# Neighbourhood attention of the last block: projection, head norm and attention woven together by pairs of heads

## The chip, the core and the metric

The kernel runs on one core of a Trainium2 chip. The metric is the device time of one launch in microseconds (us). The core has a matrix engine (TensorE, "PE" in the profile; "PEld" is its loading of stationary operands), a vector engine (DVE), an activation engine (ACT), a general engine (POOL) and a queue that issues transfers (SP). Each engine runs its own instructions in the order in which they were written; between engines only semaphores keep order. An instruction that waits on a semaphore holds up everything behind it on its engine. TensorE runs at one of two granted clocks, 2.4 or 1.2 GHz; the profile shows them as 1.00 and 0.50.

## What is computed

Two blocks of two layers each, on 512 tokens of 1024 features. The change lies in the last of the four layers: a neighbourhood attention of 16 heads with 64 features, on a grid of 64 columns by 8 rows. Each query sees a window of 16 grid columns and 256 context tokens. Cut to what matters:

```
q = rms(heads(hx @ w[:, :hd]), g_q);   k = rms(heads(hx @ w[:, hd:2*hd]), g_k);   v = heads(hx @ w[:, 2*hd:])
k_c = rms(heads(hc @ w[:, hd:2*hd]), g_k);   v_c = heads(hc @ w[:, 2*hd:])
s = [q . k_window * d**-0.5 + bias,  q . k_c * d**-0.5]        # softmax over both parts together
x = x + gx1 * (softmax(s) @ [v_window, v_c]) @ w_out
```

`rms` divides each head by the root of its mean square plus 1e-6 and multiplies by a gain.

## The kernel before

**Jobs.** Activations stand transposed, features on the 128 partitions, tokens along the row. A job is one output tile of 128 features: eight tiles k of the 1024 input features, and for each k three matmuls (high by high, high by low, low by high part, since every fp32 number is split in two fp32r halves) of 512 columns. Key and value jobs have three more of 256 columns for the context tokens. The weights of a job arrive by one transfer (`RAW`, two buffers), ACT rounds them to the high half (`round_hi`, buffer `WH`, four slots), POOL subtracts to the low half (`lo`, `WL`), PE waits for `lo_done`.

**Order of the last layer's attention.** `plan()` gives three phases of eight jobs, `na_q`, `na_k`, `na_v`, all streamed by `stream` (L1293 the 512 columns, L1295 the 256). The head norm of a finished tile is woven into later jobs: ACT squares it (L604), PE sums squares over a head with a matmul by `HALF` (`head_norm_pe`, L1273, L1276), ACT takes the root (L607, L609), DVE inverts and scales (L1587, L1589). PE turns each value tile by nine transposes (`v_turn`, L1264). Only then `neighbourhood_pe` runs the attention: 64 steps, a step being one head and 128 queries. A step has scores (L1200: three matmuls of 256 columns against local keys and three against context keys), four transposes of the numerators (`turn`, L1208) and the product with the values (`av`, L1221: four tiles, 128 columns each although a head has 64). Between them DVE adds the bias (L1804), takes the maximum (L1808), the reciprocal (L1813) and scales the result (`store`, L1818); ACT copies the context scores (L635), takes the exponential (L641) and evicts the turned numerators (L662) to `PTN`, of which there are two buffers, as there are two PSUM banks for scores, for turning and for results.

**After it.** `turn_out` turns all eight output tiles (L1008), ACT and DVE split them in halves (L667, L1834), and phase `res2` of eight jobs forms the product with `w_out`. Its first matmuls can begin at once, since the weights of its first four jobs are there.

## Time and profile before

| | us |
|---|---|
| median of 3 runs (3108.92 to 3121.93) | 3110.72 |
| profiled execution, as timed | 3116.66 |
| its span, first to last instruction | 3114.9 |
| PE busy in the span | 2893.2 (93%) |
| DVE, ACT, POOL busy | 1642.5, 1134.9, 1096.9 |

Busy means that an instruction was executing. Matmuls overlap, and their ends are modelled, so the cost of a matmul in a dense row is the distance between two starts, not its duration. The granted clock was 0.969 on average. The part that the change touches runs from the first matmul on the layer's normed input to the last of the product with `w_out`.

### The profile page before, as it was taken

The page shows a single profiled execution, that of the slowest core. Times are in us where ns is not written, and L with a number is a line of the kernel's source. Part 1 is how long each engine was busy: PE and PEld are TensorE (multiplying, and loading weights), DVE is VectorE, ACT ScalarE, POOL GpSimd, SP SyncE. Part 2 cuts the span into 40 slices and gives each one's busy share as a digit, 9 for nine tenths or more (in the row PEclk, how much of TensorE's full clock was granted, in tenths as well). Part 3 has the DMA queues.
Part 4 walks back from the last instruction along what each step waited for, and adds up shares of the span by engine and source line. Part 5 has one row for each costly group of instructions (what it writes and reads, how often), then busy time and mean ns, then how long its engine had stood idle before and what let it go on. Part 6 is the DMA issues. An engine that isn't in the chain of part 4 may idle for free.

```text
span 3114.9 us, 39241 instructions
## 1 busy us (share of the span) xinstructions
PE 2893.2 (93%) x14018; PEld 2351.2 (75%) x14018; DVE 1642.5 (53%) x2339; ACT 1134.9 (36%) x1857; POOL 1096.9 (35%) x501
## 2 busy tenths in 40 slices
PE   4998899998998899997999799999979989989998
PEld 3886588886766678874878688888858878868887
DVE  6537696755576788855212416644542565431111
ACT  3333443334464533235212423121243357542222
POOL 2441444445322444452212123233323233234443
PEclk9999899999999899998999899999979989999999
DMA  5350355523421355531111123333312110123222
GB/s 212 122 183 35 121 191 198 192 101 103 136 68 60 112 185 194 172 115 36 61 68 54 41 75 122 122 131 113 134 55 68 55 41 22 33 75 100 95 96 87
DMA packets 90419, 325.47 MB, mean 104 GB/s; under 512 B 10036, under 2 KB 12852, under 8 KB 89784
## 3 DMA queue, kind: packets, MB, share of 16 engines
q1 hardware_dynamic: 85392, 312.21, 29.3%
q10 hardware_dynamic: 4904, 11.68, 1.2%
q8 instruction: 70, 1.15, 0.2%
q14 instruction: 53, 0.43, 0.0%
HBM read 321.75 MB, written 2.10 MB: 104 GB/s over the span
## 4 chain that ended last, share of the span: by engine, by line
PE 83%; DVE 8%; ACT 4%; issue 2%; DMA 1%; POOL 1%; DVEq 0%; ACTq 0%; SPq 0%; POOLq 0%
PE bank L1293 57%; PE junk L1295 9%; PE bank L1076 2%; PE bank L1221 2%; PE bank L1061 1%; PE bank L1208 1%; PE bank L1200 1%; PE bank L1310 1%; PE bank L1180 1%; PE junk L1200 1%; ACT UF L816 1%; ACT Uh L816 1%; DVE ADA L1383 1%; PE bank L1102 1%; DMA ADA<-in_ast 1%
## 5 line engine op out<-in xcount | busy, mean ns | idle before, releaser
L466 POOL TENSOR_TENSOR WL<-RAW,WH 128x1024 fp32r<-128x1024 f32 x392 | 985.9, 2516 | 1793.0 <-ACT WH L760 1280.4
L760 ACT ACTIVATE WH<-RAW 128x1024 fp32r<-128x1024 f32 x292 | 307.3, 1053 | 384.3 <-PE junk L1295 192.0
L1293 PE MATMUL bank<-U1h,WH 128*128 128x512 f32 x960 | 378.0, 394 | 18.3 <-DVE U1l L1631 18.3
L1293 PE MATMUL bank<-Uh,WH 128*128 128x512 f32 x832 | 341.5, 410 | 56.5 <-DVE Ul L1633 56.1
L1293 PE MATMUL bank<-U1l,WH 128*128 128x512 f32 x960 | 375.4, 391 | 0.0
L1293 PE MATMUL bank<-U1h,WL 128*128 128x512 f32 x960 | 375.1, 391 | 0.0
L1293 PE MATMUL bank<-Hh,WH 128*128 128x512 f32 x864 | 340.1, 394 | 11.5 <-DVE Hl L548 11.5
L1293 PE MATMUL bank<-Hl,WH 128*128 128x512 f32 x864 | 340.7, 394 | 0.0
L1293 PE MATMUL bank<-Hh,WL 128*128 128x512 f32 x864 | 339.4, 393 | 0.0
L1293 PE MATMUL bank<-Ul,WH 128*128 128x512 f32 x832 | 333.9, 401 | 0.0
L1293 PE MATMUL bank<-Uh,WL 128*128 128x512 f32 x832 | 332.4, 400 | 0.0
L1483 DVE SCALAR_TENSOR_TENSOR XT<-bank,GATE,XT 128x512 f32 x112 | 84.0, 750 | 369.6 <-PE bank L1293 203.3
L1383 DVE CUSTOM_DVE_ANT_0 ADA<-ADA,CB 128x1024 f32<-128x1024 f32 x128 | 215.1, 1686 | 109.8 <-DMA ADA<-in_ast 98.1
L1293 PEld LDWEIGHTS bank<-Uh,WH 128*128 128x128 f32 x832 | 158.9, 191 | 108.9 <-issue 45.5
L1293 PEld LDWEIGHTS bank<-U1h,WH 128*128 128x128 f32 x960 | 181.0, 189 | 63.3 <-issue 16.1
L1293 PEld LDWEIGHTS bank<-U1h,WL 128*128 128x128 f32 x960 | 181.3, 189 | 38.3
L1293 PEld LDWEIGHTS bank<-U1l,WH 128*128 128x128 f32 x960 | 181.4, 189 | 36.5
L1293 PEld LDWEIGHTS bank<-Hh,WH 128*128 128x128 f32 x864 | 162.8, 188 | 51.4 <-DVE Hl L548 16.0
L1293 PEld LDWEIGHTS bank<-Hh,WL 128*128 128x128 f32 x864 | 162.8, 188 | 37.5
L1293 PEld LDWEIGHTS bank<-Hl,WH 128*128 128x128 f32 x864 | 163.0, 189 | 34.5
L1293 PEld LDWEIGHTS bank<-Uh,WL 128*128 128x128 f32 x832 | 159.6, 192 | 38.0
L1293 PEld LDWEIGHTS bank<-Ul,WH 128*128 128x128 f32 x832 | 159.6, 192 | 34.7
(334 smaller groups left out, 5277.4 us busy)
## 6 DMA issues: line engine op xcount, KB each, us to landing
RAW<-in_wst SPq DMA_DIRECT2D x392, 512.0 KB, 3.4
ADA<-in_ast SPq DMA_DIRECT2D x192, 512.0 KB, 4.5
NST<-in_nstrip ACTq DMA_DIRECT2D x16, 192.0 KB, 2.3
XT<-in_xt SPq DMA_DIRECT2D x1, 2048.0 KB, 15.4
STRIP<-in_strip ACTq DMA_DIRECT2D x8, 256.0 KB, 2.7
CB<-in_cb ACTq DMA_DIRECT2D x4, 512.0 KB, 4.3
DX<-in_dx ACTq DMA_DIRECT2D x1, 2048.0 KB, 8.1
out_xt<-XT SPq DMA_DIRECT2D x1, 2048.0 KB, 7.2
```

The lines of the kernel that those rows point to most:

```text
L466: pool.tensor_tensor(WL[:, s4], RAW[:, s2], WH[:, s4].bitcast(F32), ALU.subtract)\
L760: act.activation(WH[:, c % 4], RAW[:, c % 2], ACT.Copy).then_inc(S("hi_done"), 1)
L816: ins = act.activation(dst[:, t, 0:T], UF[:, t, 0:T], ACT.Identity, bias=B2[:, t, 0:1], scale=G2[:, t, 0:1])
L1061: mm = pe.matmul(BANK[VT_BANKS[half][b]][:], x[:, k, b * P:(b + 1) * P], flat(w[:, i, 4 * kk:4 * kk + 4]), start=k == 0 and m == 0, stop=k ...
L1076: mm = pe.matmul(BANK[j % 2][:], w[:, j % 4, k], x[:, k], start=k == 0 and m == 0, stop=k == KT - 1 and m == 2)
L1102: mm = pe.matmul(BANK[4 + c][:, 0:P * (b + 1)], QD[64 * c:64 * c + 64, h, b * P:(b + 1) * P], QD[64 * c:64 * c + 64, 8 + h, 0:P * (b + 1)] ...
L1200: mm = pe.matmul(BANK[bank][:, 0:256], w, x, start=m == 0, stop=m == 2)
L1221: mm = pe.matmul(BANK[6 + it % 2][:, 0:P], PTN[:, it % 2, s * P:(s + 1) * P], VN[:, tile, t * P:(t + 1) * P], start=s == 0, stop=s == 3)
L1293: mm = pe.matmul(bank_of(p, u)[:], w[:, u, k], x[:, k, 0:T], start=st and m == 0, stop=en and m == 2)
L1295: mm = pe.matmul(BANK[2 + u % 2][:, 0:C], w[:, u, k], x[:, k, T:TC], start=st and m == 0, stop=en and m == 2)
L1383: dve.tensor_tensor_reduce(tile, tile, cb[:, 0], 1.0, 0.0, ALU.mult, ALU.add, AD[:, u, 0:1])\
L1483: ins = dve.scalar_tensor_tensor(out=flat(XT[:, ds(jl, 1)]), in0=bank[:], scalar=gate_of(jl), in1=flat(XT[:, ds(jl, 1)]), op0=ALU.mult, op ...
```

## The change

`plan()` has one phase `nakqv` of 24 jobs in place of the three. The weights are laid out as key, query, value of tile 0, then of tile 1, and so on; a tile holds a pair of heads. While PE streams the three jobs of tile t, it runs the eight steps of the pair t-1 between their matmuls. The sizes of the buffers follow: keys, queries, values and outputs of two pairs stand in memory, not of eight.

- The first three jobs run side by side: for each k, the key, the query and the value matmuls, as k arrives.
- Step n of PE is: a third of the step's job units (a unit is one k of one job), `turn(n-2)`, a third, `scores(n)`, a third, `av(n-3)`. Behind it come, at fixed steps of each eight, a part of the value transposes, the head-norm sums of key and query, and the turning back of a finished pair.
- Scores are three matmuls of 512 columns (local and context keys read as one operand) into one bank, and the product with the values is of 64 columns.
- There is one bank each for scores (`BANK[3]`), turning (`BANK[5]`) and results (`BANK[6]`), and one `PTN`.
- The root of the mean square is taken as an exponential of a logarithm, with one Newton step on DVE (`root`), in place of square root and reciprocal. ACT so needs one table for the whole phase.
- Bias addition and row maximum are one DVE operation. POOL's splits of keys and queries stand between its weight splits.
- In the last eight steps PE runs the first four jobs of the product with `w_out`, k by k as output pairs finish.

```diff
+                def key_out(t):
+                    j = N_J0 + 3 * t
+                    act.wait_ge(S("pe_job"), j + 1)
...
+                    act.activation(KN[:, t % 2, NA_LOC].rearrange(rows, r=ROWS), by_row(BANK[j % 2][:]), ACT.Copy)
+                    act.activation(KN[:, t % 2, 0:C], BANK[2][:, 0:C], ACT.Copy).then_inc(S("bank_read"), 1)
...
+                    act.activation(NSQ[:], KN[:, t % 2], ACT.Square).then_inc(S("n_sq"), 1)
...
+                def turned(n):
+                    act.wait_ge(S("n_turned"), n + 1)
+                    if n >= 1:
+                        act.wait_ge(S("n_av"), n)
+                    act.activation(PTN[:], BANK[5][:], ACT.Copy).then_inc(S("n_pt"), 1)
...
+                for n in range(N_N + 2):
+                    t, s = n // 8 + 1, n % 8
+                    if s == 0 and 2 <= t <= KT:
+                        value_out(t - 1)
+                    if 1 <= n <= N_N:
+                        numerators(n - 1)
+                    if n >= 2:
+                        turned(n - 2)
+                    if s == 0 and t <= KT:
+                        round_hi(N_J0 + 3 * t + 3, (3 * t + 3) % 4)
...
+                    if n == 0:
+                        key_out(1)
+                    if s == 3 and t < KT:
+                        if t > 1:
+                            key_out(t)
+                        round_hi(N_J0 + 3 * t + 4, (3 * t + 4) % 4)
+                    if s == 4 and t < KT:
+                        key_root(t)
+                    if s == 5 and t < KT:
+                        key_hi(t)
+                        query_out(t)
+                        query_square(t)
+                    if s == 6 and t < KT:
+                        query_root(t)
+                        round_hi(N_J0 + 3 * t + 5, (3 * t + 5) % 4)
+                    if s == 6 and 2 <= t:
+                        out_hi(t - 2)
+                    if s == 7 and t < KT:
+                        query_hi(t)
...
+                for k in range(KT):
+                    pe.wait_ge(S("u_ready"), 48 + k + 1)
+                    for c in range(3):
+                        job(0, c, (k,))
+            for unit in range(3):
+                stream_part(1, unit)
+            key_ms(0)
+            for unit in range(3, 10):
+                stream_part(1, unit)
+            query_ms(0)
+            for unit in range(10, 16):
+                stream_part(1, unit)
+            for n in range(N_N + 3):
+                t, s = n // 8 + 1, n % 8
+                if t == 1:
+                    units = ((16 + s,), (), ())
+                elif t < KT:
+                    units = ((3 * s,), (3 * s + 1,), (3 * s + 2,))
...
+                if 2 <= n < N_N + 2:
+                    turn(n - 2)
...
+                if n < N_N:
+                    scores(n)
...
+                if n >= 3:
+                    av(n - 3)
+                if t <= KT and s < 3:
+                    value_turn(t - 1, s)
+                if t < KT and s == 3:
+                    key_ms(t)
+                if t < KT and s == 5:
+                    query_ms(t)
+                if 2 <= t <= KT and s == 5:
+                    turn_back(t - 2)
+            turn_back(KT - 1)
+            residual((7,), range(4))
...
+                for n in range(N_N + 4):
+                    t, s = n // 8 + 1, n % 8
+                    if n >= 4:
+                        store(n - 4)
...
+                    if n < N_N:
+                        logits(n)
+                    if 1 <= n <= N_N:
+                        sums(n - 1)
+                    if s == 4 and t < KT:
+                        root(t, 0)
+                    if s == 6 and t < KT:
+                        root(t, 1)
```

`job` waits before a key job of tile t for `bank_read` of the value job of tile t-1 (`value_out`), since both use bank 2; `av(n)` waits for `n_pt` (`turned(n)`) and for `n_o` (`store(n-1)`); `key_ms` and `query_ms` wait for `n_sq`.

**ACT around the head norm.** Before, the attention of a pair held only the steps' own work and one split of the next pair (`QNh`, `KNh`); here are two steps of it:

```order
L641 ACTIVATE PN,SM<-ZN,SM 128x512 [waits n_turned,n_max]
L624 ACTIVATE QNh_130<-QN 128x512 [waits n_score]
L625 ACTIVATE KNh<-KN 128x768
L662 ACTIVATE PTN<-bank 128x512 [waits n_av,n_turned]
L635 ACTIVATE ZN<-junk 128x256 [waits n_exp,n_score]
```

After, steps 3 to 5 of a block of eight (L795 the exponential, L803 the eviction to `PTN`, L738 to L743 `key_out`, L772 to L774 `key_root`, L785 the key split, L751 and L757 the query's copy and squares):

```order
L803 ACTIVATE PTN<-bank 128x512 [waits n_av,n_turned]
L738 ACTIVATE KN<-bank 128x8x64 [waits n_score,pe_job]
L739 ACTIVATE KN<-junk 128x256
L743 ACTIVATE NSQ<-KN 128x768 [waits n_scaled,bank_read]
L665 ACTIVATE WH<-RAW 128x1024 [waits raw_land0,pe_job]
L795 ACTIVATE ZN,SM<-ZN,SM 128x512 [waits n_z]
L803 ACTIVATE PTN<-bank 128x512 [waits n_av,n_turned]
L772 ACTIVATE NSQ<-bank,PRM 128x512 [waits n_ms]
L773 ACTIVATE NSQ<-bank,PRM 128x256
L774 ACTIVATE NSQ<-NSQ 128x768 [waits act_step]
L795 ACTIVATE ZN,SM<-ZN,SM 128x512 [waits n_z]
L803 ACTIVATE PTN<-bank 128x512 [waits n_av,n_turned]
```

The squares and the logarithm now stand behind evictions to `PTN`, and each eviction waits for `n_av`, the end of the product before it.

**PE at the end of step 5.** Before, turning and product of one step and the next scores:

```order
L1208 MATMUL bank<-IDENT,PN 128x128 x3
L1221 MATMUL bank<-VN,PTN 128x128 [waits n_o,n_pt]
L1221 MATMUL bank<-VN,PTN 128x128 x3
L1200 MATMUL bank<-KNh,QNh_131 128x256 [waits nz_done,n_zc]
```

After (L1299 and L1301 are job matmuls, L1372 the product, L1319 the query's sum of squares, L1386 the turning back):

```order
L1299 MATMUL bank<-Uh,WL 128x512
L1301 MATMUL junk<-Uh,WL 128x256
L1372 MATMUL bank<-VN,PTN 128x64 [waits n_o,n_pt]
L1372 MATMUL bank<-VN,PTN 128x64 x3
L1319 MATMUL bank<-NSQ,HALF 128x512 [waits n_scaled,n_sq]
L1386 MATMUL bank<-IDENT,ON 128x128 [waits n_scaled,n_o]
L1386 MATMUL bank<-IDENT,ON 128x128 x3
L1299 MATMUL bank<-Uh,WH 128x512
```

A sum of squares with its wait for `n_sq` now follows the product directly.

**DVE between steps 4 and 5, after** (L2040 is `store`, L2026 the bias and maximum, L2002 to L2014 are `root`). Before, no norm work stood among the stores:

```order
L2032 RECIPROCAL SM<-SM 128x1 [waits n_exp]
L2002 TENSOR_TENSOR NRT<-NSQ 128x768 [waits n_root,dve_step]
L2007 SCALAR_TENSOR_TENSOR NRT<-bank,PRM,NRT 128x512 [waits dve_step]
L2009 SCALAR_TENSOR_TENSOR NRT<-bank,PRM,NRT 128x256
L2011 SCALAR_TENSOR_TENSOR NRT<-NRT,NSQ 128x768 [waits dve_step]
L2014 SCALAR_TENSOR_TENSOR KN<-KN,SM,NRT 128x768 [waits dve_step]
L2040 TENSOR_SCALAR ON<-bank,SM 128x64 [waits n_av]
```

The store that frees the result bank stands behind the whole root.

## Rows read from the trace of the kernel before

**Rows 1.** Stretches: us; busy us (instructions) per engine; granted clock, DMA share, GB/s.
```profile
2300.40:2740.90 440.50, 420.97 (x2456) 354.98 (x2456) 209.90 (x356) 221.23 (x427) 135.16 (x96) 0.95 0.14 46
2518.60:2542.30 23.70, 12.28 (x48) 9.40 (x47) 16.13 (x20) 8.96 (x18) 8.44 (x9) 0.60 0.20 65
```

**Rows 2.** Timeline of PE at the stage's start: start us, duration us, instruction.
```profile
2300.39 0.77 PE L1293 MATMUL bank<-Uh,WH 128*128 128x512 f32 x1 [11.07 <-DVE Ul L1633]
...
2322.20 0.39 PE L1293 MATMUL bank<-Uh,WH 128*128 128x512 f32 x1
```

**Rows 3.** Timeline of PE in a value job: transposes, five units, head norm.
```profile
2464.56 1.14 PE L1264 MATMUL bank<-IDENT,TT 128*128 128x128 f32 x9
2465.46 0.48 PE L1293 MATMUL bank<-Uh,WH 128*128 128x512 f32 x1
...
2470.75 1.02 PE L1273 MATMUL bank<-NSQ,HALF 128*128 128x512 f32 x2
...
2471.86 0.58 PE L1293 MATMUL bank<-Uh,WH 128*128 128x512 f32 x1
```

**Rows 4.** Timeline of PE in one step of the attention.
```profile
2561.61 0.66 PE L1208 MATMUL bank<-IDENT,PN 128*128 128x128 f32 x4
2562.11 1.06 PE L1221 MATMUL bank<-VN,PTN 128*128 128x128 f32 x8
2563.09 0.38 PE L1200 MATMUL bank<-KNh,QNh 64*128 64x256 f32 x1
...
2563.99 0.66 PE L1208 MATMUL bank<-IDENT,PN 128*128 128x128 f32 x4
```

**Rows 5.** Instructions on tile ON: durations ns min/median/max, first and last start us.
```profile
L1818 DVE TENSOR_SCALAR ON<-bank,SM x64: 273/275/285, 2546.1 to 2692.0; 128x64 f32<-128x64 f32 x64
```

**Rows 6.** Groups by form, 2530 to 2700 us: busy us, mean ns, idle before.
```profile
L641 ACT ACTIVATE PN<-ZN,SM 128x512 f32<-128x512 f32 x64 | 45.8, 715 | 0.0
L662 ACT ACTIVATE PTN<-bank 128x512 f32<-128x512 f32 x64 | 37.6, 588 | 0.7 <-PE bank L1208 0.7
...
L641 ACT ACT_TABLE_LOAD x1 | 1.3, 1283 | 0.0
```

**Rows 7.** Groups by form, 2280 to 2530 us, same columns.
```profile
L466 POOL TENSOR_TENSOR WL<-RAW,WH 128x1024 fp32r<-128x1024 f32 x25 | 61.0, 2440 | 186.9 <-ACT WH L691 123.1 <-ACT WH L760 63.8
...
L607 ACT ACTIVATE NRS<-bank,PRM 128x512 f32<-128x512 f32 x16 | 11.0, 689 | 71.6 <-PE bank L1276 41.4 <-PE bank L1273 30.2
...
L903 ACT ACTIVATE KN<-bank 128x512 f32<-128x512 f32 x8 | 9.5, 1191 | 16.5 <-PE junk L1295 16.5
...
L760 ACT ACTIVATE WH<-RAW 128x1024 fp32r<-128x1024 f32 x8 | 8.6, 1078 | 0.0
...
L1589 DVE SCALAR_TENSOR_TENSOR KN<-KN,PRM,NRS 128x768 f32<-128x768 f32 x7 | 7.1, 1019 | 0.2
L604 ACT ACTIVATE NSQ<-KN 128x768 f32<-128x768 f32 x8 | 6.6, 828 | 0.0
...
L1589 DVE SCALAR_TENSOR_TENSOR QN<-QN,SM,NRS 128x512 f32<-128x512 f32 x8 | 6.0, 752 | 0.3
...
L604 ACT ACTIVATE NSQ<-QN 128x512 f32<-128x512 f32 x8 | 4.9, 618 | 0.0
...
L609 ACT ACTIVATE NRS<-bank,PRM 128x256 f32<-128x256 f32 x8 | 3.7, 467 | 0.0
```

**Rows 8.** Timeline of PE: first and last matmul of the product with w_out.
```profile
2697.33 0.47 PE L1293 MATMUL bank<-OH,WH 128*128 128x512 f32 x1
...
2740.75 0.39 PE L1293 MATMUL bank<-OH,WL 128*128 128x512 f32 x1
```

**Rows 9.** A stretch at the end of layer 1's attention, columns of rows 1.
```profile
978.00:982.00 4.00, 0.66 (x4) 0.42 (x4) 2.28 (x9) 0.77 (x2) 0.00 (x0) 0.82 0.00 0
```

**Rows 10.** Timeline of PE just after it.
```profile
982.80 0.79 PE L1091 MATMUL bank<-OH,WH 128*128 128x512 f32 x1 [2.23 <-DVE OL L1766]
...
987.23 0.48 PE L1091 MATMUL junk<-OL,WH 128*128 128x512 f32 x1
```

More of the change, by code:

```diff
@@ new lines, in key_ms, with query_ms @@
+            def key_ms(t):
+                pe.wait_ge(S("n_sq"), 2 * t + 1)
+                if t >= 1:
+                    pe.wait_ge(S("n_scaled"), 2 * t)
+                    pe.wait_ge(S("vn_out"), 3 * t)
+                pe.matmul(BANK[4][:], HALF[:], NSQ[:, NA_LOC], start=True, stop=True)
+                pe.matmul(BANK[7][:, 0:C], HALF[:], NSQ[:, 0:C], start=True, stop=True).then_inc(S("n_ms"), 1)
+            def query_ms(t):
+                pe.wait_ge(S("n_sq"), 2 * t + 2)
+                pe.wait_ge(S("n_scaled"), 2 * t + 1)
+                pe.matmul(BANK[4][:], HALF[:], NSQ[:, 0:T], start=True, stop=True).then_inc(S("n_ms"), 1)
@@ new lines, in scores @@
+            def scores(n):
+                h, b = divmod(n, 4)
+                t, i = h // 2, h % 2
+                r, q = slice(64 * i, 64 * i + 64), slice(b * P, (b + 1) * P)
+                if n % 8 == 0:
+                    pe.wait_ge(S("n_lo"), 2 * t + 2)
+                if n == 0:
+                    pe.wait_ge(S("bank_read"), N_J0 + 3)
+                else:
+                    pe.wait_ge(S("n_z"), n)
+                keys = na_keys(t, b)
+                passes = ((QNh[r, t % 2, q], KNh), (QNh[r, t % 2, q], KNl), (QNl[r, t % 2, q], KNh))
+                for m, (w, x) in enumerate(passes):
+                    mm = pe.matmul(two(BANK[3][:]), w, two(x[r, keys]), start=m == 0, stop=m == 2)
+                mm.then_inc(S("n_score"), 1)
@@ new lines, in turn, with av @@
+            def turn(n):
+                pe.wait_ge(S("n_exp"), n + 1)
+                if n >= 1:
+                    pe.wait_ge(S("n_pt"), n)
+                for q in range(4):
+                    mm = pe.transpose(BANK[5][:, q * P:(q + 1) * P], ZN[:, n % 2, q * P:(q + 1) * P], IDENT[:])
+                mm.then_inc(S("n_turned"), 1)
+            def av(n):
+                h, b = divmod(n, 4)
+                t, i = h // 2, h % 2
+                pe.wait_ge(S("n_pt"), n + 1)
+                if n % 8 == 0:
+                    pe.wait_ge(S("vn_out"), 3 * t + 3)
+                if n >= 1:
+                    pe.wait_ge(S("n_o"), n)
@@ new lines, in residual @@
+            def residual(ks, us):
+                for k in ks:
+                    pe.wait_ge(S("o_ready"), 24 + k + 1)
+                    for u in us:
+                        if k == 0:
+                            pe.wait_ge(S("lo_done"), N_RES + u + 1)
+                            pe.wait_ge(S("bank_read"), N_RES)
+                            if u == 3:
+                                pe.wait_ge(S("n_scaled"), 2 * KT)
+                        for m, (w, x) in enumerate(((WH, OH), (WH, OL), (WL, OH))):
+                            mm = pe.matmul(BANK[(0, 1, 2, 4)[u]][:], w[:, u, k], x[:, k], start=k == 0 and m == 0, stop=k == KT - 1 and m == 2)
+                        if k == KT - 1:
+                            mm.then_inc(S("pe_job"), 1)
@@ new lines, in sums, with store @@
+                def sums(n):
+                    dve.wait_ge(S("n_exp"), n + 1)
+                    link(dve.reciprocal(SM[:, 24 + n % 4:25 + n % 4], SM[:, 16 + n % 4:17 + n % 4]))
+                def store(n):
+                    h, b = divmod(n, 4)
+                    dve.wait_ge(S("n_av"), n + 1)
+                    if n % 8 == 0 and n >= 16:
+                        dve.wait_ge(S("n_back"), n // 8 - 1)
+                    dve.tensor_scalar(ON[:, h // 2 % 2, b, h % 2 * NHD:(h % 2 + 1) * NHD], BANK[6][:, 0:NHD],
+                                      SM[:, 24 + n % 4:25 + n % 4], None, ALU.mult).then_inc(S("n_o"), 1)
@@ L1957, in layout @@
     mlp(0)
-    st += [jobs(i["na_w_qkv_2"][0], every, range(24)), jobs(i["na_w_out_2"][0], every, range(KT))]
+    st += [jobs(i["na_w_qkv_2"][0], every, [c for t in range(KT) for c in (8 + t, t, 16 + t)]), jobs(i["na_w_out_2"][0], every, range(KT))]
     mlp(1)
```

537 lines of the change are left out of this document (282 added, 255 removed).

## The prediction

> **What bounds the kernel now.** I read the stretches of the stage first. From 2300.40 to 2740.90 us PE is busy 421.0 of 440.5 us, DVE 209.9, ACT 221.2, POOL 135.2 [rows 1]. So PE sets the time of this stage, and the three others have room, if their work falls where PE needs it. Then I read PE's timeline at the stage's two weak places. At the start the first job goes at the pace at which the norm delivers its input, and the granted clock is at half until 2322.20 [rows 2]; the first 21.8 us hold one job and nine matmuls, 33 in all, or 7.5 us of dense work (0.227 us each, below). That leaves 14.3 us to be had. Between the last value job and the steady attention, from 2518.60 to 2542.30, PE is busy 12.3 of 23.7 us at a clock of 0.60 [rows 1]; the work in it (a norm, nine transposes, four score groups, two turns) is 6.6 us at the prices below, so 17.1 us are lost. Last, the attention itself: the 64 stores begin between 2546.1 and 2692.0 [rows 5], 2.32 us per step, and in a step PE has no gap worth naming [rows 4]. The attention is not waiting for anything; it costs what its matmuls cost.
>
> **Prices on PE**, as distances of starts. The product with w_out is 64 units of three 512-column matmuls from 2697.33 to 2740.75 [rows 8]: 43.65 us with the last one's 0.23, 0.68 a unit, 0.227 a matmul, 5.46 a job. Five units with context columns take 2465.46 to 2470.75 [rows 3], 1.06 each, 8.46 a job. Nine transposes 0.95, the key's sum of squares 1.11 and a late first matmul, so 1.25 [rows 3]; the query's has 512 of its 768 columns, 0.85. A step: turn 0.50, product 0.98, scores 0.90 [rows 4]; scaled to the mean of 2.32 I take 0.45, 0.97, 0.90. The new scores have the same 1536 columns in three matmuls instead of six, so 0.69 to 0.90; I keep 0.90, since every step now changes between more kinds of matmul.
>
> **The narrow product.** It has 64 columns instead of 128. The eight starts of one product lie 0.11 to 0.12 us apart (1.06 us for eight, the last lasting 0.275) [rows 4]. The trace has no fp32 product of 64 columns, so the bounds are half the price, 0.49, if columns set it, and 0.97 if the loading of the stationary operand does, of which there are as many as before. I take 0.97, the nearest row, and keep 0.49 for the range. The Trainium skill has a rule on each side. "TensorE: Matmul & The Clock Gate", section "Back-to-back issue gap", gives about 60 cycles for 1 to 64 columns, by which the product would fall to half and the stage lose 31 us. The same page, section "LDWEIGHTS (loading the stationary operand)", has the load follow the number of columns of the weights over 1.2 GHz, 107 ns for 128, by which nothing is gained; no row here tells the two apart, since 128 fp32 columns cost about the same.
>
> **PE's work after the change, without waits.** Three first jobs 5.46 + 2 x 8.46 = 22.4, plus one rise of the clock, 2.2 (from 982.80 to 987.23 PE ran at half speed after a pause [rows 10], so 4.4 us did the work of 2.2): 24.6. Dense three-job work outlasts the norm's delivery. Jobs 4 and 5 with both sums of squares: 8.46 + 5.46 + 1.25 + 0.85 = 16.0. Block 1, where each of eight steps has one unit: 8 x (1.06 + 0.90) + 6 x 0.45 + 5 x 0.97 + 0.95 + 1.25 + 0.85 = 26.3. Blocks 2 to 7: 22.4 + 8 x 2.32 + 0.95 + 1.25 + 0.85 + 0.45 = 44.5 each, 267 together. Block 8: 24 x 0.68 + 18.6 + 1.4 = 36.3. The end: eight units, two turns, three products, one turning back, 9.8, and four jobs, 21.8: 31.6. Sum 401.8 against 440.6 now. If no wait came in, 38.8 us would be gained: the 14.3 less 2.2, the 17.1, and small change.
>
> **The waits in a block.** All rests on one row of the order: ACT's `turned(n-2)` waits for `n_av`, so for `av(n-3)`, which PE runs at the very end of step n. What ACT has behind it in that step starts only when PE's step is over. And PE waits for three of these things right there. I walk through one of blocks 2 to 7; 0.2 is what a matmul takes beyond its slot, and back-to-back ACT operations overlap by 0.1.
> 1. Step 3: product ends, eviction 0.59 [rows 6], key copy 1.19, context copy about 0.4 (0.47 for a 256-wide ACT operation), squares 0.83 [rows 7]. `key_ms` comes right behind the product: PE waits 3.05.
> 2. Step 4 ends; eviction 0.59, logarithms 0.69 and 0.47, exponential 0.83; DVE's root, 1.0 + 0.65 + 0.47 + 1.02 + 1.02 = 4.2, priced by the scaling rows of 768 and 512 [rows 7]; then the store 0.28 [rows 5] that frees the result bank. That is 7.2 us after the end of step 4. The next product is reached 0.68 + 0.45 + 1.06 + 0.90 + 1.06 = 4.15 us after it (0.1 more for a turn that comes early). PE waits 2.95.
> 3. That product ends; eviction 0.59, key split 0.83, query copy 1.19, squares 0.62 [rows 6, 7], and `query_ms` is next: PE waits 3.3.
> 4. Step 6 ends; eviction, logarithm 0.69, exponential 0.62, DVE 0.7 + 3 x 0.75 = 3.0 [rows 7], store: 5.4 us against 4.5 of PE work up to the product of step 7. PE waits 0.9.
> 5. That product ends; eviction, query split 0.62, value copies 1.19 + 0.4. The next block's first matmul waits for them: 2.7. With 0.2 for two turns behind a short unit the sum is 13.1 a block.
>
> Six blocks: 78.6. Block 1 has no wait of point 1, but its steps are short, 2.4 us up to the product: 4.8 + 3.3 + 3.1 + 2.7 = 13.9. Block 8 has no norm; 1.2 for turns behind short units.
>
> **The waits at the start and end.** ACT's row after the first jobs is long: key copies and squares 2.4, table load 1.28 [rows 6], query copy 1.2, value copies 1.6, rounding 1.08, logarithm and exponential 2.0; then DVE 4.2, key split 0.8, query squares 0.6. It begins 1.7 us before the three jobs end, so `query_ms(0)` is free 14 us after, while PE has 11.1 us to do: 2.9 of wait. Then query norm 1.4 + 3.1 + 0.6, POOL's query split (half of a weight split, 1.2) and weight split 2.44 [rows 7] until the sixth job may start: 9.0 against 4.1 of work, a wait of 5.0. At the end the chains of the last two steps cost 1.6, store, turning back and the two splits 2.6, and the fifth job's weights, rounded behind the first residual's squares, 3.2. Before, these weights came hidden under 43 us of dense matmuls. Together 7.9 + 7.4 = 15.3.
>
> **The clock.** From 978 to 982 us PE was busy 0.66 of 4 us and the granted clock had begun to fall; the next matmul, after another pause of 2.23, ran at half [rows 9, 10]. Points 2 and 3 make the same picture in every block: 3 us of wait, one of work, 3.3 of wait. I count one fall a block and one at the start, 8 x 2.2 = 17.6.
>
> **Sum.** 401.8 + 13.9 + 78.6 + 1.2 + 15.3 + 17.6 = 528.4 us, against 440.6: 87.8 us more. The profiled execution took 3116.66 us, so 3204.5; it was 5.9 above the median of the runs, so **3198.5** to be compared with 3110.72.
>
> **Rivals.**
> - *The step is long enough.* If the norm's chain did not stand between two PE steps (if the eviction of `PTN` fell in mid-step, say, by the product being done earlier than I place it), only the waits at the start and end would remain: 401.8 + 15.3 + 1.2 = 418.3, 22.3 us faster, 3088. For it: DVE and ACT are half idle [rows 1]. Against it: the order of the instructions and the semaphore; it decides from the point at which ACT reaches `key_out` 3 us before PE reaches `key_ms`.
> - *The narrow product is cheap.* 64 x 0.48 = 31 us less, since the product lies on every chain: 3168. For it: half the columns; against it: as many loads.
> - *The clock stays down longer.* At the stage's start PE was at half for 21.8 us though it worked two thirds of the time [rows 2]. If each block lost 11 us instead of 2.2, the sum grows by 62: 3260. If it fell at points 1 and 5 too, the sum would grow by 2 x 2.2 x 7 = 31: 3229. [...] Against the long fall: behind each pause here stands dense work.
> - *The waits are half of what I walk*, because copies overlap more: 3150.
>
> **How the numbers follow.** Forecast 0.60; narrow product cheap 0.16; clock down longer 0.13; half the waits 0.06; waits hidden 0.05. The range 3145 to 3240 takes in the second and the fourth and leaves out 3260 and what is below, some 0.15. Half a per cent, 15.6 us, is about what a measurement of this kernel can tell from no change. Slower by more 0.93; within it 0.02, a mix of half waits and cheap product; faster by more 0.05.
>
> **What would show it.** Right: PE waits on ACT's squares at both sums of squares (some 3 us, 15 times together), on DVE's store at the product of steps 5 and 7, and on ACT's value copy at a block's first matmul; blocks of 58 to 60 us; clock dips once a block; first three jobs done some 25 us after the stage's start. Wrong: blocks near 45 us, or the fp32 loads of the product 0.06 apart.

## The result and the profile after

The changed kernel takes 3261.5 us (median of 4 runs, 3256.9 to 3266.8) beside 3109.8 us for the kernel before on the same chip: a ratio of 1.0468, interval 1.0444 to 1.0493. I had forecast 3198.5 with a range of 3145 to 3240. The direction was right; the loss is 152 us where I had 88.

The stage of the change runs from 2289.6 to 2884.1 us of the profiled execution (span 3256.9 us). Its stretches: us; busy us and instructions of PE, PE's loads, DVE, ACT, POOL; granted clock, DMA share, GB/s.

```profile
2289.60:2884.10 594.50, 484.47 (x2264) 370.86 (x2264) 176.94 (x397) 212.79 (x378) 134.12 (x96) 0.84 0.11 34
2389.60:2800.00 410.40, 330.14 (x1554) 251.41 (x1554) 113.39 (x270) 136.85 (x253) 85.79 (x66) 0.82 0.09 29
```

The first row answers to the first of [rows 1]: 594.5 us in place of 440.5, with fewer matmuls, and a clock of 0.84 in place of 0.95. My sum for it was 528.4. The second row is blocks 2 to 7, each from the start of one value copy to the next: 68.4 us a block, of which PE stands idle 13.4. I had written 59.8, with 13.1 of waits. What PE waited for in the six blocks (total us, times, longest):

```profile
PE bank L1372 <- DVE ON L2040: 28.7, 12, 2.5
PE bank L1319 <- ACT NSQ L757: 18.7, 6, 3.1
PE bank L1312 <- ACT NSQ L743: 16.9, 6, 2.8
PE bank L1299 <- ACT TV L767: 15.3, 6, 2.6
```

These are the five points of the forecast: the two products that wait for the store, the query's sum of squares, the key's, and the block's first matmul. Point 1 can be read off the timeline of PE, ACT and DVE (start, duration, instruction, idle time before it and its releaser):

```profile
2620.24 1.00 PE L1372 MATMUL bank<-VN,PTN 128*128 128x64 f32 x8
2621.33 0.60 ACT L803 ACTIVATE PTN<-bank 128x512 f32<-128x512 f32 x1 [3.48 <-PE bank L1372]
2621.33 0.28 DVE L2040 TENSOR_SCALAR ON<-bank,SM 128x64 f32<-128x64 f32 x1 [1.01 <-issue]
2621.82 1.08 ACT L738 ACTIVATE KN<-bank 128x512 f32<-128x512 f32 x1
2622.68 0.43 ACT L739 ACTIVATE KN<-junk 128x256 f32<-128x256 f32 x1
2623.15 0.84 ACT L743 ACTIVATE NSQ<-KN 128x768 f32<-128x768 f32 x1
2623.90 1.04 ACT L665 ACTIVATE WH<-RAW 128x1024 fp32r<-128x1024 f32 x1
2624.04 2.07 PE L1312 MATMUL bank<-NSQ,HALF 128*128 128x512 f32 x2 [2.81 <-ACT NSQ L743]
```

ACT stood idle 3.48 us, though the key tile was complete, since its next instruction is the eviction, which waits for this step's product. Only then come copy, context copy and squares, and PE waits 2.81 us for them (forecast 3.05). The 2.07 us of the sum itself are twice what they are at full clock. The granted clock around this pause, in stretches of 2 us:

```profile
2620.00:2622.00 2.00, 1.23 (x10) 1.05 (x8) 0.60 (x4) 0.67 (x2) 0.00 (x0) 1.00 0.00 0
2622.00:2624.00 2.00, 0.00 (x0) 0.00 (x0) 0.00 (x0) 1.97 (x4) 0.00 (x0) 0.64 0.00 0
2624.00:2626.00 2.00, 1.96 (x3) 0.92 (x4) 0.00 (x0) 1.64 (x3) 0.99 (x1) 0.50 0.00 0
2626.00:2628.00 2.00, 2.00 (x6) 1.46 (x5) 0.00 (x0) 0.00 (x0) 1.36 (x1) 0.50 0.03 8
2628.00:2630.00 2.00, 2.00 (x9) 1.50 (x7) 0.00 (x0) 0.00 (x0) 0.00 (x0) 0.66 0.72 205
```

It falls in the pause and is back late in the last stretch: by the shares, 1.4 + 2 + 2 + 1.4 = 6.8 us at 1.2 GHz. The same picture stands at the pair of waits of step 5 (half from about 2640 to 2650, 10.2 us) and at the block's start (from about 2595 to 2602, 6.8 us):

```profile
2640.00:2648.00 8.00, 4.88 (x16) 3.46 (x16) 0.54 (x4) 3.65 (x6) 3.86 (x4) 0.50 0.00 0
2596.00:2602.00 6.00, 5.36 (x17) 4.47 (x18) 0.00 (x0) 1.19 (x4) 2.70 (x4) 0.50 0.01 3
```

So **a block has three falls**, where I had counted one. All six blocks have them at the same places, some 24 us of each block at the lower clock.

Outside the six blocks the stage takes 184.1 us, where I had 169.6. After the stage nothing has changed (373.9 us to the end of the span before, 372.8 after). Ahead of it the profiled execution is 10.8 us shorter than that of before; this isn't put down to the change (last section).

### The profile page after: what moved, and what is told of

Read it like the earlier page. It is cut to its first block, busy times and chain, and to the rows that moved or that the text cites. A ratio compares the mean times of both kernels' runs of the same rounds, so it can differ in the third digit from the quotient of the medians.

```text
span 3256.9 us, 38601 instructions
## 1 busy us (share of the span) xinstructions
PE 2945.5 (90%) x13826; PEld 2363.0 (73%) x13826; DVE 1616.4 (50%) x2380; ACT 1126.3 (35%) x1809; POOL 1089.6 (33%) x502
## 4 chain that ended last, share of the span: by engine, by line
PE 80%; DVE 9%; ACT 6%; issue 3%; DMA 1%; POOL 1%; DVEq 0%; ACTq 0%; SPq 0%; POOLq 0%
PE bank L1502 50%; PE junk L1504 7%; PE bank L1299 4%; PE bank L1178 2%; PE bank L1372 2%; PE junk L1348 1%; PE bank L1163 1%; PE junk L1301 1%; PE bank L1282 1%; PE bank L1519 1%; PE bank L1357 1%; DVE NRT L2011 1%; DVE ADA L1591 1%; PE bank L1204 1%; DMA ADA<-in_ast 1%
## 5 line engine op out<-in xcount | busy, mean ns | idle before, releaser
L876 ACT ACTIVATE WH<-RAW 128x1024 fp32r<-128x1024 f32 x276 | 290.2, 1052 | 380.6 <-PE junk L1504 188.1
L1502 PE MATMUL bank<-Uh,WH 128*128 128x512 f32 x640 | 256.4, 401 | 40.4 <-DVE Ul L1823 39.8
L1591 DVE CUSTOM_DVE_ANT_0 ADA<-ADA,CB 128x1024 f32<-128x1024 f32 x128 | 224.7, 1762 | 109.0 <-DMA ADA<-in_ast 97.4
L1502 PE MATMUL bank<-Ul,WH 128*128 128x512 f32 x640 | 253.2, 396 | 0.0
L1502 PE MATMUL bank<-Uh,WL 128*128 128x512 f32 x640 | 252.4, 394 | 0.0
L1502 PEld LDWEIGHTS bank<-Uh,WH 128*128 128x128 f32 x640 | 121.2, 189 | 76.7 <-issue 31.8
L803 ACT ACTIVATE PTN<-bank 128x512 f32<-128x512 f32 x64 | 38.2, 597 | 331.8 <-PE bank L1372 331.3
L665 ACT ACTIVATE WH<-RAW 128x1024 fp32r<-128x1024 f32 x116 | 121.7, 1051 | 79.3 <-DMA RAW<-in_wst 50.8
```

What stands on the lines that cost most here:

```text
L665: act.activation(WH[:, u], RAW[:, u % 2], ACT.Copy).then_inc(S("hi_done"), 1)
L803: act.activation(PTN[:], BANK[5][:], ACT.Copy).then_inc(S("n_pt"), 1)
L876: act.activation(WH[:, c % 4], RAW[:, c % 2], ACT.Copy).then_inc(S("hi_done"), 1)
L1502: mm = pe.matmul(bank_of(p, u)[:], w[:, u, k], x[:, k, 0:T], start=st and m == 0, stop=en and m == 2)
L1591: dve.tensor_tensor_reduce(tile, tile, cb[:, 0], 1.0, 0.0, ALU.mult, ALU.add, AD[:, u, 0:1])\
```

## The experiments

In the table a block is a sixth of the time from the second value copy to the eighth; idle is PE's idle time in it. Ratios are to the kernel before in the same comparison, with their intervals; its medians there were 3115.9 (the four rows from e1_fill to b_av64), 3116.1 (the four from b_late64 to c2_best) and 3122.8 (the last three, each one run and so without a ratio).

| | launch us | ratio | block us | idle us | clock in blocks |
|---|---|---|---|---|---|
| changed kernel | 3261.5 | 1.0468 | 68.4 | 13.4 | 0.82 |
| e1_fill | 3219.3 | 1.0317 (1.0280 to 1.0354) | 60.3 | 1.5 | 1.00 |
| e2_two | 3129.1 | 1.0032 (1.0012 to 1.0052) | 47.4 | 1.3 | 0.99 |
| e3_order | 3141.9 | 1.0077 (1.0047 to 1.0107) | 49.5 | 2.6 | 0.98 |
| b_av64 | 3227.6 | 1.0346 (1.0313 to 1.0378) | | | |
| b_late64 | 3107.8 | 0.9986 (0.9963 to 1.0009) | | | |
| h_av128 | 3253.9 | 1.0461 (1.0428 to 1.0493) | 65.6 | 13.5 | 0.88 |
| c1_steady | 3113.2 | 0.9998 (0.9979 to 1.0016) | 45.6 | 0.0 | 0.99 |
| c2_best | 3093.4 | 0.9938 (0.9920 to 0.9956) | 45.2 | 0.0 | 1.00 |
| f1_pause1 | 3239.4 | | 62.4 | 3.9 | 0.96 |
| f2_pause23 | 3229.4 | | 62.4 | 6.5 | 0.94 |
| f3_pause45 | 3239.1 | | 62.6 | 6.0 | 0.94 |

### What the clock costs: the waits filled with useless matmuls

My theory after the result: the waits are as forecast, and the clock that they bring down makes up most of what was missed. The rival: a block holds more work, or dearer work, than I had priced.

```diff
+            def fill(count, j, start=False):
+                if start and count:
+                    pe.wait_ge(S("bank_read"), j - 1)
+                for _ in range(count):
+                    pe.matmul(BANK[j % 2][:, 0:256], ZR[:], Uh[:, 0, 0:256], start=start, stop=start)
...
+                if 2 <= t < KT and s == 5:
+                    fill(20, N_J0 + 3 * t + 2)
                 if n >= 3:
                     av(n - 3)
```

`ZR` is a tile of zeros; the other four places are filled alike, with 20 or 22.

> The changed kernel; in blocks 2 to 7 PE does useless matmuls (256 columns of zeros added to an open sum) where it stood waiting, 20 to 22 at each of the five places of a block, some 2.3 us each place; the results don't change. In the changed kernel a block takes 68.4 us: 13.5 of waits and some 15 of work at half clock, which loses 7 to 8 us. Theory (the waits cost twice, once as idle time and once through the clock they bring down): the clock stays at 1.00 in blocks 2 to 7, a block falls to about 61 us although nothing is taken out of it, the launch to about 3215 us. Rival (a block is long because of its work and its waits, and the clock is a small part, 2.2 us as forecast): block above 66 us, launch above 3245.

Blocks 2 to 7 together, and what PE still waits for in them:

```profile
2402.00:2763.90 361.90, 353.18 (x2162) 287.69 (x2160) 113.49 (x270) 137.94 (x253) 86.63 (x66) 1.00 0.11 34
```
```profile
PE bank L1328 <- ACT NSQ L759: 3.1, 6, 0.5
PE bank L1321 <- ACT NSQ L745: 2.5, 6, 0.4
PE bank L1301 <- ACT TV L769: 0.9, 5, 0.2
```

608 matmuls more, and 48.5 us less. Nothing that the kernel needs was taken out, and the waits are still there, only full. So **8.1 us of each block's 68.4 are the clock**, against 2.2 in my sum. It is rather a lower bound: at the two products no wait is left, so the filling may outlast it there, and this profile has the slower pace of the last section (up to 0.4 us of a block).

### What makes the waits: ACT's row

Two ways to untie ACT from the end of PE's step. The first gives `PTN` a second buffer (in the place of the last output tile, which is written only at the end):

```diff
-        PTN = at("PTN", [T], A_B + 61 * KB)
+        PTN = (at("PTN0", [T], A_B + 61 * KB), at("PTN1", [T], A_B + 14 * KB))
...
-                    if n >= 1:
-                        act.wait_ge(S("n_av"), n)
-                    act.activation(PTN[:], BANK[5][:], ACT.Copy).then_inc(S("n_pt"), 1)
+                    if n >= 2:
+                        act.wait_ge(S("n_av"), n - 1)
+                    act.activation(PTN[n % 2][:], BANK[5][:], ACT.Copy).then_inc(S("n_pt"), 1)
```

> The changed kernel with two buffers for the turned numerators (PTN), so that ACT's eviction of step n waits for the product before the last one and no longer for the one at the end of the same step. Theory (ACT's row stands behind the end of PE's step, and all five waits come from that): ACT begins its extra work 1.7 us into a step, the waits at both sums of squares and at the products go, only 0.7 us remain at a block's start (the value copy needs the last value unit), the clock stays up: block 68.4 to about 48 us, block 1 some 10 us less, launch about 3130 us. Rival (ACT and DVE have too much to do in steps 3 to 7 whichever way they are tied): half of the waits stay, with their clock falls, block 58 to 60 us, launch about 3200.

The second leaves one buffer and moves one line:

```diff
                     if 1 <= n <= N_N:
                         numerators(n - 1)
-                    if n >= 2:
-                        turned(n - 2)
                     if s == 0 and t <= KT:
                         round_hi(N_J0 + 3 * t + 3, (3 * t + 3) % 4)
...
                     if s == 7 and t < KT:
                         query_hi(t)
+                    if n >= 2:
+                        turned(n - 2)
```

> The changed kernel with one line moved: in each step ACT does its extra work (key and query copies, squares, logarithms, splits, rounding) ahead of the eviction of the turned numerators instead of behind it. One PTN buffer, all else as it was. Theory (the order behind the eviction makes the waits): four of the five waits of a block go and the one at the block's start stays, since the value copy still stands behind the eviction, 2.7 us and one fall of the clock: block about 51 us, launch about 3150 us. Rival (the chain between two PE steps is too long in any order, since the eviction still starts only when the step is over): the waits move to the turning (BANK[5]) and the block stays above 60 us, launch above 3210.

What PE waits for in blocks 2 to 7, first with two buffers, then with the line moved:

```profile
PE bank L1319 <- ACT NSQ L757: 4.7, 6, 0.8
PE bank L1299 <- ACT TV L767: 3.3, 5, 0.7
```
```profile
PE bank L1299 <- ACT TV L767: 12.2, 6, 2.0
PE bank L1319 <- ACT NSQ L757: 2.5, 6, 0.4
```

Both did what the theory wanted: 47.4 us a block (48 expected) and 49.5 (51 expected), and the launch falls by 4.4 and 3.9 of the 4.7 per cent that the change had cost. With the line moved the store's waits are gone too, since DVE's root now gets its exponential in mid-step; what stays is the block's start, as expected. So the waits come from the place of one instruction in ACT's row, and not from the amount of work on ACT or DVE.

### The narrow product

```diff
-                    mm = pe.matmul(BANK[6 + it % 2][:, 0:P], PTN[:, it % 2, s * P:(s + 1) * P], VN[:, tile, t * P:(t + 1) * P],
+                    mm = pe.matmul(BANK[6 + it % 2][:, 0:NHD], PTN[:, it % 2, s * P:(s + 1) * P], VN[:, tile, h * NHD:(h + 1) * NHD],
```

(DVE's store reads the 64 columns where they now lie.)

> The kernel before, with the product of each step taken over the 64 value columns of its head instead of the 128 of the pair; nothing else changes. In its 64 steps a step takes 2.32 us with 0.98 for the product's eight passes. If the columns set the price, the product falls to about half and the launch by 31 us, to 3079. If the loading of the stationary operand sets it, nothing changes, 3110. The changed kernel's trace has 0.83 for a product at full clock, by which 0.15 us a step go: 9 to 10 us less, 3100.

None of the three came: the launch is 112 us longer. The stretch in which the attention stands (same columns as above), and one of its products with the scores behind it:

```profile
2560.00:2780.00 220.00, 220.00 (x941) 202.24 (x940) 71.38 (x208) 92.56 (x221) 45.25 (x51) 0.50 0.04 12
```
```profile
2601.49 1.80 PE L1221 MATMUL bank<-VN,PTN 128*128 128x64 f32 x8
2603.23 0.58 PE L1200 MATMUL bank<-KNh,QNh 64*128 64x256 f32 x1
```

PE is busy in all of the 220 us, without a pause, and the clock stays at its lower level; the product takes 1.74 us up to the scores, where it took 0.98 [rows 4]. In the kernel before the clock had also been down ahead of the attention (0.60 [rows 1]) and rose when it began. The next run asks whether the narrow product brings the clock down or only keeps it there. It is wide up to step 15 and narrow from step 16 on:

```diff
-                    mm = pe.matmul(BANK[6 + it % 2][:, 0:P], PTN[:, it % 2, s * P:(s + 1) * P], VN[:, tile, t * P:(t + 1) * P],
+                    mm = pe.matmul(BANK[6 + it % 2][:, (h % 2 * NHD if it >= 16 else 0):((h % 2 + 1) * NHD if it >= 16 else P)], PTN[:, it % 2, s * P:(s + 1) * P],
+                                   VN[:, tile, (h * NHD if it >= 16 else t * P):((h + 1) * NHD if it >= 16 else (t + 1) * P)],
```

> The kernel before, with the narrow product (64 columns) only from step 16 of its 64 steps on, that is after the granted clock has come up. With the narrow product in all 64 steps the launch took 3227.6 us: PE had no pause from step to step, and the clock stayed at 0.50 over 240 us. Two readings. A: steps with the narrow product only keep a low clock from rising, and do not bring a high one down: then 48 steps cost 0.15 us less each, launch 7 us below the kernel before. B: they bring it down by themselves, without a pause: then 48 steps of 4.2 us in place of 2.3, launch some 90 us above the kernel before, and the clock falls soon after step 16.

```profile
2520.00:2545.00 25.00, 18.51 (x77) 16.57 (x78) 12.15 (x24) 11.66 (x25) 13.00 (x13) 0.50 0.05 17
2545.00:2560.00 15.00, 15.00 (x113) 13.46 (x113) 8.23 (x24) 9.91 (x25) 2.10 (x3) 0.99 0.05 15
...
2600.00:2640.00 40.00, 40.00 (x307) 36.13 (x306) 23.29 (x70) 29.09 (x73) 16.63 (x18) 1.00 0.08 21
```
```profile
2641.57 1.00 PE L1221 MATMUL bank<-VN,PTN 128*128 128x64 f32 x8
2642.50 0.38 PE L1200 MATMUL bank<-KNh,QNh 64*128 64x256 f32 x1
...
2643.89 1.00 PE L1221 MATMUL bank<-VN,PTN 128*128 128x64 f32 x8
2644.83 0.38 PE L1200 MATMUL bank<-KNh,QNh 64*128 64x256 f32 x1
```

The clock comes up under the wide product and stays up under the narrow one: the first reading. At full clock the narrow product costs 0.93 us and a step 2.33, against 0.98 and 2.32: half the columns, nothing gained. The launch (0.9986) can't be told from the kernel before, so the 7 us that I had put on it aren't shown either. The Trainium skill, "TensorE: Matmul & The Clock Gate", section "Back-to-back issue gap", would have the product at half; for this fp32 product the row shows that it isn't so, and the section "LDWEIGHTS (loading the stationary operand)", by which the load of 128 columns goes on costing the same, fits it at full clock. That section has no clock in its rule, but at the lower clock the same product took 1.74 us.

Does that matter in the changed kernel, whose clock falls three times a block and has to come back among narrow products? There the product is made wide (the store reads its half of the result):

```diff
-                    mm = pe.matmul(BANK[6][:, 0:NHD], PTN[:, q * P:(q + 1) * P], VN[:, t % 2, tile, i * NHD:(i + 1) * NHD],
+                    mm = pe.matmul(BANK[6][:, 0:P], PTN[:, q * P:(q + 1) * P], VN[:, t % 2, tile],
```

> The changed kernel with the product over 128 value columns (the pair's) in place of 64, as in the kernel before; one of the two halves is read. At full clock a product costs some 0.15 us more, 64 of them 10 us: if the width bears on nothing else, 3271 us. If the narrow product also delays the clock's rise after each pause, the wide one shortens the stretches at half (23 us of a block's 68.4 now), and the launch falls below 3250 in spite of the larger product.

```profile
2391.10:2784.50 393.40, 312.53 (x1554) 238.29 (x1554) 113.30 (x270) 136.86 (x253) 85.99 (x66) 0.88 0.09 31
```

The waits are the same to 0.2 us in total, the products are twice as wide, and the blocks are 2.8 us shorter, at a clock of 0.88 in place of 0.82: some 15.5 us of a block at the lower clock in place of 24. Most of the difference is at point 1. The wait for the key's squares is 2.81 us as before, but it brings the clock down in one of the six blocks only; here it stands in block 5 (from 2615.95 to 2618.76), without a fall:

```profile
2616.00:2618.00 2.00, 0.00 (x0) 0.00 (x0) 0.28 (x1) 1.92 (x4) 0.00 (x0) 1.00 0.00 0
2618.00:2620.00 2.00, 1.24 (x5) 0.73 (x5) 0.00 (x0) 2.00 (x3) 0.27 (x1) 1.00 0.00 0
```

So with the wide product the same waits cost less clock. That the width itself does it isn't shown: with other lengths of the blocks the waits also come at other moments, and no run keeps these apart. The launch didn't reach the bound that I had set for it (3250), and the ratios 1.0461 and 1.0468 can't be told apart. So even the difference rests on one profiled execution of each, both at the same pace (last section): 17 us less in the six blocks, 12.8 us less in the whole span (3244.1 us). For the launch it isn't shown.

### What one fall costs

The filled kernel again, with the filling left out at one place, or one pair of places, at a time:

```diff
-                        fill(20, N_J0 + 3 * t + 1)
+                        fill(0, N_J0 + 3 * t + 1)
                     key_ms(t)
```

> The kernel with filled waits (block 60.3 us, clock 1.00 throughout), with the filling taken out at one place of a block: the wait for the key's squares, 2.8 us, in otherwise dense work. Theory (each pause brings the clock down on its own, and the work behind it then runs at half for some 4.6 us, as the changed kernel's trace has it there): a block 2.3 us longer, 62.6. Rival (one pause alone does not do it, it takes the pauses together): 60.3 and the clock at 1.00.

> The same with the filling taken out at the two waits of step 5, before the product and before the query's sum, which stand one product apart. Theory: one fall for the two, 6.8 us of work at half as in the changed kernel's trace, a block 3.4 us longer, 63.7. My forecast's price for this pair was 2.2 us, 62.5. Rival (two falls): 4.5 us or more, above 64.8.

> The same with the filling taken out at the waits of step 7's product and of the next block's first matmul. Theory: one fall, 5.4 us of work at half as in the changed kernel's trace, a block 2.7 us longer, 63.0; the three runs together then make up the 8.1 us by which the filled waits shortened a block. Rival (pauses work together over a longer stretch): the three together well below 8.

Blocks of 62.4, 62.4 and 62.6 us against 60.3: **each pause or pair of pauses costs 2.1 to 2.3 us of clock by itself**, the pair no more than the single one. The first is what its theory gave (2.3); the other two cost less than theirs (3.4 and 2.7), which I had taken from the changed kernel's low stretches. The three make 6.4 us, not 8.1. Each is one run, so this rests on the profiled blocks. The stretches around point 1 in the first of them, in block 3 and in block 7:

```profile
2494.90:2496.90 2.00, 1.62 (x11) 1.35 (x11) 0.98 (x4) 0.29 (x1) 0.00 (x0) 1.00 0.00 0
2496.90:2498.90 2.00, 0.00 (x0) 0.00 (x0) 0.00 (x0) 1.97 (x4) 0.00 (x0) 1.00 0.00 0
2498.90:2500.90 2.00, 1.57 (x3) 0.82 (x4) 0.00 (x0) 2.00 (x4) 0.60 (x1) 0.78 0.00 0
2500.90:2502.90 2.00, 2.00 (x7) 1.44 (x5) 0.00 (x0) 0.03 (x1) 1.75 (x1) 0.50 0.00 0
2502.90:2504.90 2.00, 2.00 (x10) 1.45 (x9) 0.00 (x0) 0.00 (x0) 0.00 (x0) 0.87 0.47 121
```
```profile
2745.00:2747.00 2.00, 0.60 (x1) 0.50 (x2) 0.00 (x0) 1.97 (x4) 0.00 (x0) 0.69 0.00 0
2747.00:2749.00 2.00, 2.00 (x5) 0.98 (x3) 0.00 (x0) 1.00 (x3) 1.63 (x1) 0.50 0.00 0
2749.00:2751.00 2.00, 2.00 (x7) 1.51 (x7) 0.00 (x0) 0.00 (x0) 0.72 (x1) 0.50 0.14 33
2751.00:2753.00 2.00, 2.00 (x7) 1.22 (x6) 0.00 (x0) 0.00 (x0) 0.00 (x0) 0.60 0.60 229
```

After the same 2.8 us of pause the clock is down for 0.9 + 2 + 0.5 = 3.4 us in block 3 and for 1.2 + 2 + 2 + 1.6 = 6.8 in block 7, with the same instructions around it; blocks 4 to 6 are as block 3, block 2 as block 7. In the changed kernel it is 6.8 in every block. So the other pauses of a block aren't needed for the long fall, and what decides when the clock comes back, these runs don't settle. (The second run's profile has the quicker pace of the last section, which is worth up to 0.4 us of a block, so its price may be 2.5 and the sum of the three 6.8.)

### A version that beats both

From the two buffers: in step 5 the query's copy and squares go ahead of the key split on ACT, and in step 7 PE runs the last value unit ahead of the scores.

```diff
-                        key_hi(t)
                         query_out(t)
                         query_square(t)
+                        key_hi(t)
...
+                if 2 <= t < KT and s == 7:
+                    units = (units[0], units[1] + units[2], ())
```

> The changed kernel with two buffers for PTN (as before, block 47.4 us) and two rows of order more: in step 5 ACT takes the query copy and its squares ahead of the key split (PE waited up to 1.0 us for the squares), and in step 7 PE runs the last value unit ahead of the scores, so that the value copy has 1.7 us before the next block (PE waited 0.7). Theory (what is left in a block is these two waits and dense work): block 46.0 us, launch 8 us below the version with the two buffers alone, about 3121. Rival (these waits are replaced by the next one on the same chain, the store behind the root): block 47.2, launch as that version, 3128.

In blocks 2 to 7 PE is now busy without a gap, and no wait is left in them:

```profile
2392.30:2665.70 273.40, 273.40 (x1552) 216.41 (x1553) 110.69 (x269) 142.86 (x254) 89.23 (x66) 0.99 0.14 45
```

The blocks came out at 45.6 us (46.0 expected), which is what a block's dense work costs; I had priced it at 44.5. Last, the opening in another order (cut to ACT's part; `key_square` is the squares taken out of `key_out`):

```diff
+                act.preload_act_table_set("natural_log_exp_and_others")
                 key_out(0)
-                act.dma_start(NMK[:], a["nmask"]).then_inc(S("nmask_land"), 16)
-                for h in range(2):
-                    load_nstrip(act, h)
-                act.preload_act_table_set("natural_log_exp_and_others")
                 query_out(0)
+                key_square(0)
                 value_out(0)
+                act.dma_start(NMK[:], a["nmask"]).then_inc(S("nmask_land"), 16)
+                for h in range(2):
+                    load_nstrip(act, h)
                 round_hi(N_J0 + 4, 0)
+                round_hi(N_J0 + 5, 1)
                 key_root(0)
-                key_hi(0)
                 query_square(0)
+                key_hi(0)
                 query_root(0)
+                key_out(1)
                 query_hi(0)
-                round_hi(N_J0 + 5, 1)
+                key_square(1)
```

> The one before, and the opening put in another order: ACT loads its table before the first jobs end, copies the query before it squares the key, rounds the sixth job's weights at once; POOL splits them before the keys; the value tiles of pair 0 are turned ahead of the attention; pair 1's key norm begins in step 1 instead of 4. In the version with two buffers PE stood 3.6 us before the fourth job, 1.0 at the query's sum, 4.8 before the sixth job's weights and 2.7 at a product, with two or three falls of the clock of 2 us. Theory (these are order, not work): 10 us of the waits and two falls go, launch about 14 us below the one with the steady blocks mended, 3107, beside 3116 of the kernel before. Rival (the norm's chain of pair 0, 14 us on ACT, DVE and POOL in turn, is the bound whichever way it is written): at most the 2.6 us of the fourth job, 3118.

```profile
2288.50:2711.40 422.90, 412.35 (x2264) 325.05 (x2264) 175.93 (x397) 219.97 (x378) 139.26 (x96) 0.99 0.15 48
```

The same 2264 matmuls as in the changed kernel take 422.9 us in place of 594.5. The launch is 0.62 per cent below the kernel before (0.80 to 0.44), some 19 us, more than the 9 us that I had expected of it. The stage is 17.6 us below the 440.5 of the kernel before, where I had put 38.8 on all of the waits going. Of the 21 us between, 10.6 are idle time that PE still has (422.9 less 412.4), 4 are the dense blocks (45.2 in place of 44.5); the rest isn't split.

## Why the prediction was off, point by point

**The bound and the chain: right.** PE sets the time; `turned(n-2)` behind `n_av` holds ACT's row until PE's step is over. Moving that one line, or giving it a second buffer, took away the waits that the prediction had put down to it.

**The waits: right.** A block has 13.4 us of idle time against 13.1 forecast: key squares 2.8 (3.05), the query's 3.1 (3.3), the block's start 2.6 (2.7), the product of step 5 2.5 (2.95). Step 7's product, forecast at 0.9, waits about 2.3 (28.7 us in twelve waits, less six of 2.5). What was mis-sized there is one operation of DVE's root for the query: priced at 0.75, it took 2.34 us in each of the six blocks, each time beside a weight split on POOL:

```profile
2657.24 2.38 POOL L481 TENSOR_TENSOR WL<-RAW,WH 128x1024 fp32r<-128x1024 f32 x1 [10.21 <-ACT WH L665]
2657.83 2.34 DVE L2011 SCALAR_TENSOR_TENSOR NRT<-NRT,NSQ 128x512 f32<-128x512 f32 x1
```

With the line moved (e3_order) the split is over before that operation starts, and it takes 0.69 us in every block. So the close sum is partly luck: four points came 0.1 to 0.45 us lower than forecast, one 1.4 higher. In block 1 no key wait, as forecast. At full clock the waits are worth 60.3 - 45.6 = 14.7 us a block, with what the filling outlasts them. Missed was one at the opening: 3.6 us before the fourth job, for the query copy behind key copies, squares and table load.

**The price of PE's work: 1.1 us a block short.** Dense blocks measure 45.6, not 44.5. It isn't the products, which take 0.81 to 0.84 us up to the next matmul at full clock where I had 0.97. That the changes between kinds of matmul cost a little each is my guess and not shown.

**The narrow product: right to keep the price of the wide one.** 0.93 for 0.98 in the kernel before, and no shorter step; in the changed kernel 0.81 to 0.84 narrow and 0.81 to 0.89 wide (h_av128), from start to the next matmul. The rival at 3168 falls.

**The clock: the step that failed.** It was the term "one fall a block and one at the start, 8 x 2.2 = 17.6". The price of a fall that stands alone was right (2.1 to 2.3 measured). The number was wrong: points 1 and 5, which I had left out without a reason of their own though I had some 3 us of wait at each, bring the clock down as points 2 and 3 do. And together the falls of a block cost 8.1 us where singly they make 6.4; why, is open. The rival "the clock stays down longer" had both halves in it, as alternatives: falls at points 1 and 5 too (3229), or longer ones (3260); it took some of each. That the launch measured 3261.5 beside its 3260 is luck: of the 8.8 us a block that it added for the clock 5.9 came, and other terms made up the rest. The Trainium skill, "TensorE: Matmul & The Clock Gate", section "HAM oscillation — how this bites in real kernels", describes a throttled stretch behind every pause, but for pauses longer than any in these blocks. Here the measurement decides: pauses of 2.8 us brought the clock down too.

**The sum.** The stage is 66.1 us over my 528.4. Six blocks at 68.4 instead of 59.8 are 51.6 of it: clock 6 x 5.9 = 35.4, waits at full clock 6 x 1.6, dense work 6 x 1.1. The other 14.5 lie about half in the opening and block 1, where 3.6 is the wait that I missed and the clock was 0.78 in block 1, and half behind the six blocks. There the clock was 0.90 over 52.0 us and 0.89 over the next 31.9, where I had put no fall; by an estimate from these two rows (0.10 x 52.0 + 0.11 x 31.9) that is up to 8.7 us. I haven't split it further.

**The range.** It left out the case that came, at 0.13, because I had treated the clock as a rival instead of as a count: each wait in the list should have been asked whether a fall follows it.

## What to carry to other kernels

When PE waits 2.5 us or more in otherwise dense work, count 2 us of lost clock on top for each place where that happens, and more where a block has several (8.1 us for three here). It is a mean, not a law: a pause of 2.8 us cost no fall in five of six blocks with the wide product, and the pauses of 2.0 us that the moved line left brought the clock down in two of the blocks. The way to price it is to fill the pauses with useless matmuls and look at what is left. Where an engine's row holds one instruction that waits for the end of another engine's step, put the rest of that step's work ahead of it, or give it a second buffer: here one moved line took back 3.9 of the 4.7 per cent. Before making a matmul narrower, see what its load costs, and whether the clock has yet to come up at that place.

## What the runs showed of the hardware that I had not expected

- **A row of matmuls without a pause can stay at the lower clock.** With 64 columns instead of 128 in eight of a step's eighteen matmul passes, PE was busy 220 of 220 us at 1.2 GHz; with the clock brought up first, the same row kept 2.4 GHz. So this row keeps whichever of the two clocks it starts with.
- **The same pause doesn't always cost the same.** A wait of 2.8 us with the same instructions around it was followed by 3.4 us at the lower clock in four blocks and 6.8 in two (f1_pause1).
- **One operation of DVE took 2.3 us beside POOL's weight split and 0.69 without it** (above, point by point). It reads both of its inputs from SBUF; the one ahead of it, which has one from PSUM, ran beside the same split in its usual 0.75 us.
- **Dense rows have two paces at one clock.** Stretches of the preceding layer, which all these kernels share, first of the kernel before, then of the changed one:

```profile
1800.00:2200.00 400.00, 400.00 (x2265) 346.74 (x2264) 194.57 (x237) 90.66 (x120) 125.82 (x47) 1.00 0.34 115
```
```profile
1800.00:2200.00 400.00, 400.00 (x2309) 349.65 (x2309) 205.47 (x241) 93.18 (x124) 124.33 (x48) 1.00 0.34 118
```

  2265 or 2309 matmuls in 400 us, both at a clock of 1.00; all the profiles of this study have the one number or the other, to within one. It doesn't look like a matter of the kernel: f1_pause1 and f2_pause23 differ only in where they are filled, and have one pace each. The version with two buffers ran three times at 3116 to 3117 us and seven times at 3128 to 3136; that these two groups are the two paces fits, but isn't shown, as each kernel has one profile. The seven profiles of the slower pace reach the stage at 2299.8 to 2308.3 us, the six of the quicker at 2288.5 to 2295.4. The kernel before has the slower pace and the changed one the quicker, and so the latter is 10.8 us ahead before the stage begins. This is why I compared stages by blocks and launches by ratios of medians.
